# Attention whose value products are batched and turned round, page numbers clamped once, and streams that are never read

## What is computed

```python
def sb_attend(q, q_pos, k, v, k_pos):
    z = jnp.einsum('bthd,bshd->bhts', q, k).astype(jnp.float32) * HEAD_DIM ** -0.5
    mask = k_pos[None, :] < q_pos[:, None]
    log_1m = jnp.where(mask, jax.nn.log_sigmoid(-z), 0.0)
    suffix = lax.cumsum(log_1m, axis=3, reverse=True) - log_1m
    a = jnp.where(mask, jnp.exp(jax.nn.log_sigmoid(z) + suffix), 0.0)
    return jnp.einsum('bhts,bshd->bthd', a.astype(v.dtype), v)
...
    o_nsa = gates[..., 0:1] * o_cmp + gates[..., 1:2] * o_slc + gates[..., 2:3] * o_win
    mix = jnp.concatenate([rms_norm(o_nsa, g_on), rms_norm(o_sb, g_os)], axis=2).reshape(B, T, MIX_WIDTH)
    h = x + mix @ w_out
```

## Time and profile before

| | |
|---|---|
| runs | 3027.76, 3020.37 and 2997.0 us, median 3020.37 |
| profiled execution | 3020.68 us, of it a span of 3018.6 us from the first to the last instruction |
| mean granted clock of TensorE | 0.860 |
| busy over the span | TensorE 2675.0 us (89%), VectorE 1256.2 (42%), ScalarE 798.2 (26%), GpSimd 831.3 (28%) |
| attend, 682 to 1849 us | TensorE 1080.55 us busy at clock 0.75, VectorE 652.25, ScalarE 361.35, GpSimd 562.54 |
| decode_nsa, 1849 to 2040 us | TensorE 73.06 us busy at clock 0.65, VectorE 42.87, GpSimd 48.56 |

### The profile page before, as it was taken

How to read it: one execution, slowest core, us unless ns; L and a number is a source line. 1 busy time by engine, 2 the same in 40 slices (tenths; PEclk the granted TensorE clock), 3 DMA queues, 4 the chain that set the end, 5 groups by cost and what they waited for, 6 DMA issues and landing times. The chain is left out here.

```text
span 3018.6 us, 45708 instructions
## 1 busy us (share of the span) xinstructions
PE 2675.0 (89%) x13736; PEld 2003.8 (66%) x13736; DVE 1256.2 (42%) x2483; ACT 798.2 (26%) x1487; POOL 831.3 (28%) x845
## 2 busy tenths in 40 slices
PE   7989699983999999999999994357989999999999
PEld 6778677772765554555555551133469999999999
DVE  3463233332656566555566650223321111114553
ACT  4232133321333333332233330001121111113332
POOL 0120244403545545454455440412200000000000
PEclk9999789995569787776688797678999999999999
DMA  4224654408245545444465346313121111113200
GB/s 143 93 88 138 159 135 129 126 21 172 85 116 157 144 127 161 135 138 122 129 162 157 119 125 219 71 43 119 57 78 47 47 45 48 46 35 111 67 29 24
DMA packets 269781, 314.28 MB, mean 104 GB/s; under 512 B 62465, under 2 KB 177986, under 8 KB 269354
## 3 DMA queue, kind: packets, MB, share of 16 engines
q1 hardware_dynamic: 238842, 266.46, 30.3%
q0 software_dynamic: 14528, 38.32, 5.1%
q10 hardware_dynamic: 16192, 6.93, 0.9%
HBM read 278.89 MB, written 37.44 MB: 105 GB/s over the span
## 5 line engine op out<-in xcount | busy, mean ns | idle before, releaser
L1070 POOL TENSOR_TENSOR late<-late 128x512 f32<-128x512 f32 x256 | 336.7, 1318 | 280.3 <-DMA late<-in_cache_sb_kv 246.5
L1995 PE MATMUL pg<-h_turned_hi,w_gu_hi 128*128 128x344 f32 x1056 | 338.5, 321 | 10.2 <-DVE h_turned_lo L2043 10.2
L1997 PE MATMUL pg<-h_turned_hi,w_gu_lo 128*128 128x344 f32 x1056 | 338.4, 320 | 0.0
L1996 PE MATMUL pg<-h_turned_lo,w_gu_hi 128*128 128x344 f32 x1056 | 338.2, 320 | 0.0
L1190 PE MATMUL decode_ps<-late,weights_dec 128*8 128x512 f32 x512 | 312.6, 714 | 9.2 <-DMA late<-in_cache_sb_kv 8.0
L1241 ACT ACTIVATE probs<-scores,minus_max 128x63 f32<-128x63 f32 (+4 forms) x192 | 109.6, 571 | 604.2 <-DVE minus_max L1314 574.4
L2121 PE MATMUL py<-w_down_hi,act_hi 128*128 128x256 f32 x792 | 225.7, 285 | 9.8 <-DVE w_down_lo L2168 9.8
L2038 DVE TENSOR_TENSOR w_gu_lo<-late,w_gu_hi 128x512 fp32r<-128x512 f32 x88 | 61.0, 693 | 401.9 <-ACT w_gu_hi L2008 401.9
L2122 PE MATMUL py<-w_down_lo,act_hi 128*128 128x256 f32 x792 | 225.0, 284 | 0.0
L2123 PE MATMUL py<-w_down_hi,act_lo 128*128 128x256 f32 x792 | 225.0, 284 | 0.0
L2104 POOL DMA_DIRECT2D out_y_prompt<-y_rows x32 | 17.4, 545 | 744.5 <-DVE y_rows L2156 744.5
(11 more groups left out here) (281 smaller groups left out, 5360.0 us busy)
## 6 DMA issues: line engine op xcount, KB each, us to landing
late<-in_cache_sb_kv SPq DMA_DIRECT2D x512, 256.0 KB, 2.9
late<-in_w_gate_up SPq DMA_DIRECT2D x88, 256.0 KB, 2.9
late<-in_cache_nsa_kv SPq DMA_DIRECT2D x160, 128.0 KB, 3.8
late<-in_cache_nsa_kv POOLq DMA_DIRECT2D x96, 128.0 KB, 3.3
late<-in_w_down SPq DMA_DIRECT2D x4, 2816.0 KB, 10.9
w_in_raw<-in_w_in SPq DMA_DIRECT2D x40, 256.0 KB, 4.8
x_sb<-in_x_prompt SPq DMA_DIRECT2D x8, 512.0 KB, 3.9
out_sb_p<-proj_sb SPq DMA_DIRECT2D x16, 256.0 KB
```

The source lines that it names most:

```text
L1070: eng.tensor_tensor(prod[:, p % NPR], kr[:, p % RING], qb[:, u], ALU.mult).then_inc(multiplied, 1)
L1995: eng.matmul(pg[:, e, c, 0:CW], w_hi[:, h, j, :], hT_hi[:, k, cols], start=k == 0, stop=False)
L1996: eng.matmul(pg[:, e, c, 0:CW], w_hi[:, h, j, :], hT_lo[:, k, cols], start=False, stop=False)
L1997: mm = eng.matmul(pg[:, e, c, 0:CW], w_lo[:, h, j, :], hT_hi[:, k, cols], start=False, stop=k == KT - 1)
```

## The change

attend is written anew, and page numbers are treated differently in three stages.

- The loop is unrolled, and the order is that of BLOCK: 16 steps of two heads (u) and two neighbouring tiles (a), 16 blocks, 264 iterations.
- The values now stand in the array (64 columns) and the turned probabilities stream, 128 columns for sb and 256 for the others (two heads or two tiles of queries). Two products write rows 0 to 63 and rows 64 to 127 of `out_ps`: z is the head for sb, sel or win for the others, the tile for cmp. Five batches to a block, cut into pieces at the iterations of PV_AT. ScalarE copies a finished batch (`copy_out`), TensorE transposes it back (`turn_back`), VectorE scales it into `mix` (`finish`). The denominators come from the exponential's own sum (accum_out) instead of a 65th column.
- A value page of the samples is multiplied with weights padded to 32 columns, and four pages write rows 0 to 31, 32 to 63, 64 to 95 and 96 to 127 of `decode_ps`; the mask `diag` and the final sum run over 128 rows. The value ring has eight pages. Pages are spread over all 256 steps by a cost of each step (DEC), the last sample's value pages among them.
- `keep_streaming`: after the scores of each step of at most 512 columns (all of cmp, the others for tiles 0 to 3, 160 of 256 steps) two products of 384 columns, identity times masks, go into columns 512 to 895 of the same half of `scores`. Nobody reads them.
- VectorE saves one group of transposes in three, ScalarE two (before, half each). Queries are loaded in blocks of 256 columns by GpSimd, and v_sb by GpSimd instead of SyncE.
- SyncE loads eight page numbers at a time and doesn't check them. In compress VectorE clamps the page table once; in decode_nsa it clamps the block numbers; the checks of SyncE, ScalarE and GpSimd in these stages go.
- The copies of win_s_out move from decode_nsa to SyncE's queue in attend (sample 0, page 16), and the kv_win loads of decode_nsa behind ScalarE's first exponentials.

The diff, cut to its core:

```diff
-            _, numbers = nc.values_load_multi_w_load_instructions(pt[0:1, at + ids[0]:at + ids[-1] + 1], engines=[eng.engine], min_val=0, max_val=NPOOL - 1)
+            _, numbers = nc.values_load_multi_w_load_instructions(pt[0:1, at + ids[0]:at + ids[-1] + 1], engines=[eng.engine], min_val=0, max_val=NPOOL - 1, skip_runtime_bounds_check_because=CLAMPED)
...
+                eng.tensor_copy(ptf[:, :], pt[:, :])
+                eng.drain()
+                eng.tensor_scalar(ptf[:, :], ptf[:, :], 0.0, float(NPOOL - 1), ALU.max, ALU.min)
+                eng.drain()
+                eng.tensor_copy(pt[:, :], ptf[:, :]).then_inc(table_set, 1)
...
-        vr = late[:, 2048:4096].rearrange("p (r n) -> p r n", r=RING)
...
+        value_slot = lambda p: (vr_low, vr_high)[p % VRING // 4][:, p % 4]
...
-        aw = sb("weights_dec", [P, NH, NPAGE])
+        aw = sb("weights_dec", [P, 32, NPAGE])
...
+        BLOCK = [(0, 0, "sb"), (0, 0, "cmp"), (1, 0, "cmp"), (0, 1, "cmp"), (1, 0, "sb"), (1, 1, "cmp"), (0, 0, "sel"), (1, 0, "sel"),
+                 (0, 1, "sb"), (0, 0, "win"), (1, 0, "win"), (0, 1, "sel"), (1, 1, "sb"), (1, 1, "sel"), (0, 1, "win"), (1, 1, "win")]
+        STEPS = [(N, u, 2 * k + a, kind) for N in range(NBODY) for k in range(4) for u, a, kind in BLOCK]
...
-        KPAGES, VPAGES = spread((2, 2, 3, 4, 5, 5, 5, 6)), spread((0, 3, 3, 4, 5, 5, 6, 6))
...
-            body(0, 0)
-            with eng.Fori(1, 3) as i:
-                body(i, i - 1)
-            body(3, 1)
-            for s in range(H):
-                tail(s)
...
+        NBATCH = 5 * U // 16
+        PV_AT, OUT_AT = ((8,), (10, 11), (12, 13, 14), (18, 19), (20, 21, 22)), (9, 12, 15, 20, 23)
+        END = U - 16 + OUT_AT[4] + 1
...
+        cost = [0.9 + 0.4 * tiles_of(kind, t) for N, u, t, kind in STEPS]
+        DEC = [[] for _ in range(END)]
+        for n in range((NH + 1) * NPAGE):
+            goal, i, total = (n + 0.5) / ((NH + 1) * NPAGE) * sum(cost), 0, cost[0]
+            while total < goal:
+                i += 1
+                total += cost[i]
+            DEC[i].append((n // NPAGE, n % NPAGE))
+        VGROUP = {6: 0, 9: 1, 13: 2, 16: 3, 20: 4, 23: 5, 27: 6, 31: 7}
...
+                def numbers(h, p):
+                    _, found = nc.values_load_multi_w_load_instructions(pt[0:1, h * NPAGE + p:h * NPAGE + p + 8], engines=[eng.engine], min_val=0, max_val=NPOOL - 1, skip_runtime_bounds_check_because=CLAMPED)
+                    return found
...
-                    page = eng.value_load(pt[0:1, bass.ds(h * NPAGE + p, 1)], min_val=0, max_val=NPOOL - 1)
...
+                for h in range(NH + 1):
+                    for p0 in range(0, NPAGE, 8):
+                        key_ids = numbers(h, p0) if h < NH else None
+                        value_ids = numbers(h - 1, p0) if h else None
+                        for p in range(p0, p0 + 8):
+                            if h < NH:
+                                key_page(h, p, key_ids[p - p0])
+                            if h:
+                                value_page(h - 1, p, value_ids[p - p0])
+                            if p == 5 and h >= 2:
                                 store_row(h - 2)
-                            if p == 6 and not zero(h) and not (isinstance(h, int) and h == NH - 1):
-                                eng.wait_ge(pv_done, h * H)
-                                load_values(h + 1, 1 - u)
-
-                def tail(s):
-                    value_page(NH - 1, s)
-                    if s == 5:
-                        store_row(NH - 2)
-
-                turns(eng, body, tail)
+                            if p == 16 and h == 0:
+                                eng.dma_start(io["win_s_out"][:, 0:WINDOW - 1, :], io["state"][:, 1:WINDOW, :]).then_inc(row_stored_w, 16)
...
+                def keep_streaming(f):
+
+                    if width(STEPS[f][3], STEPS[f][2]) <= 512:
+                        for _ in range(2):
+                            eng.matmul(S[:, f % 2, 512:512 + 3 * P], identb[:, :], masks[:, :, :].rearrange("p m q -> p (m q)"), start=True, stop=True)
...
-                        mm = eng.matmul(O[:, 0:HD if kind == "sb" else HD + 1], l, r, start=c == 0, stop=c == tiles - 1)
...
+                def turn_back(bt):
+                    N, t, kind, W = batch(bt)
+                    eng.wait_ge(ot_saved, bt + 1)
+                    bank_free(("out", bt))
+                    for u in range(W // P):
+                        mm = eng.transpose(PT[:, bank_of["out", bt], u * P:(u + 1) * P], oT[:, bt % 2, u * P:(u + 1) * P], ident[:, :])
+                    mm.then_inc(out_turned, 1)
...
+                    count = (t + 1, t + 1 if kind == "sb" else tiles_of("win", t))
+                    for c in range((t + 1) * piece // pieces, (t + 1) * (piece + 1) // pieces):
+                        for z in range(2):
+                            if c >= count[z]:
+                                continue
+                            if kind == "sb":
+                                l, r = vs[:, z, c, :], prT[:, SB_SLOT + c, z * P:z * P + P]
+                            else:
+                                name = ("sel", "win")[z]
+                                l, r = vx[:, z, first_tile(name, t) + c, kv, :], prT[:, slot_of(name, t) + c, :]
+                            mm = eng.matmul(O[HD * z:HD * z + HD, 0:W], l, r, start=c == 0, stop=c == count[z] - 1)
...
-                            eng.matmul(DB[0:NH, :], aw[:, :, NPAGE - 1 - p], vr[:, p % RING], start=p == 0, stop=p == NPAGE - 1).then_inc(v_used, 1)
...
+                        for p in pages:
+                            eng.wait_ge(v_loaded[p % VRING], h * VPER - VPER + 16 * (p // VRING) + 16)
+                        for i, p in enumerate(pages):
+                            eng.matmul(DB[32 * i:32 * i + 32, :], aw[:, :, NPAGE - 1 - p], value_slot(p), start=p < SIDE, stop=p >= NPAGE - SIDE).then_inc(v_used, 1)
...
+                for i in range(END):
+                    if i < U:
+                        scores(i)
+                        keep_streaming(i)
+                    for bt, _ in at_iteration(i, OUT_AT):
+                        turn_back(bt)
+                    if 2 <= i < U + 2:
+                        transposes(i - 2)
+                    for bt, piece in at_iteration(i, PV_AT):
+                        product(bt, piece)
+                    for h, s in DEC[i]:
+                        sample(h, s)
...
-                    eng.activation(pr[:, s % 2, 0:w], S[:, s % 2, 0:w], ACT.Exp, bias=nm[:, s:s + 1]).then_inc(exp_done, 1)
...
+                    eng.activation(pr[:, f % 2, 0:w], S[:, f % 2, 0:w], ACT.Exp, bias=nm[:, f % 8:f % 8 + 1], accum_out=den[:, t, u, br:br + 1]).then_inc(exp_done, 1)
...
+                def copy_out(bt):
+                    N, t, kind, W = batch(bt)
+                    eng.wait_ge(pv_done, bt + 1)
+                    if bt >= 2:
+                        eng.wait_ge(out_turned, bt - 1)
+                    eng.activation(oT[:, bt % 2, 0:W], O[:, 0:W], ACT.Copy).then_inc(ot_saved, 1)
...
-                    eng.reciprocal(f, O[:, HD:HD + 1])
...
+                    eng.reciprocal(f4, den[:, t, :, 1:3])
...
-            _, found = nc.values_load_multi_w_load_instructions(block_id[0:1, 32 * b + a:32 * b + e], engines=[eng.engine], min_val=0, max_val=2 * NPOOL - 1)
+            _, found = nc.values_load_multi_w_load_instructions(block_id[0:1, 32 * b + a:32 * b + e], engines=[eng.engine], min_val=0, max_val=2 * NPOOL - 1, skip_runtime_bounds_check_because=CLAMPED)
...
-                eng.dma_start(io["win_s_out"][:, 0:WINDOW - 1, :], io["state"][:, 1:WINDOW, :]).then_inc(o_stored, 16)
-                eng.dma_start(io["win_s_out"][:, WINDOW - 1, :], io["win_new"]).then_inc(o_stored, 16)
...
-                for b in range(NB):
-                    eng.dma_start(wk[:, b], io["state"][b].rearrange("(t p) e -> p t e", p=P)).then_inc(state_loaded[b // SIDE], 16)
...
+                for b in range(NB):
+                    eng.dma_start(wk[:, b], io["state"][b].rearrange("(t p) e -> p t e", p=P)).then_inc(state_loaded[b // SIDE], 16)
...
-                eng.tensor_copy(block_id[:, :], PB[0:1, 256:256 + X * 16]).then_inc(ids_set, 1)
+                eng.tensor_scalar(idf[:, :], PB[0:1, 256:256 + X * 16], 0.0, float(2 * NPOOL - 1), ALU.max, ALU.min)
+                eng.drain()
+                eng.tensor_copy(block_id[:, :], idf[:, :]).then_inc(ids_set, 1)
```

640 lines of the change are left out of this document (342 added, 298 removed).

## The result

The changed kernel takes 2837.38 us (median of five runs, 2814.77 to 2844.85) against 3020.37 us: a ratio of 0.9412, 95% interval 0.9363 to 0.946. The forecast was 2641 us with a range of 2530 to 2830. The direction was right; the gain was 183 us instead of 379. The profiled execution is the shortest of the five, with a span of 2813.1 us, so sums within the profile come out some 22 us shorter than the median, and where the loop of another run is laid beside this one, that much of the difference belongs to this execution.

What follows compares the result with a forecast made beforehand. TensorE and its clock were taken to bound the loop. Loop -294, setup -8, tail -35, decode_nsa -40 and compress -3 sum to -380; 3018.6 - 380 + 2.1 = 2641 us, range 2530 to 2830.

Steps and rivals of the forecast that it cites:

- the loop's sum: Attention loop: TensorE's 677 us of work times 1.12 for waits, plus 27 us for the clock, gives 785 us.
- one block's 27 us for the clock: Attention loop: the first blocks still run at 1.2 GHz; one block's 27 us of work was put on that.
- the rule on weight loads: TensorE: weight loads overlap products only in different row groups; column tiles share theirs, so much of both gains would be lost.
- the range 629 to 725: Attention loop: TensorE's work at full clock after the change, 677 us with half the cost of changes of shape.
- the 183 from 860 to 677: Attention loop: TensorE's work at full clock falls from 860 us, eight heads of 107.5 us, to 677 us.
- the 48 us for changes of shape: Attention loop: 240 visits to column tiles, two shape changes each, cost TensorE 0 to 96 us; half was taken.
- rival A: Attention loop: streams don't hold the clock, blocks of tiles 0 to 3 stay at 1.2 GHz; +193, 2834 us; chance 0.14.
- rival D: Attention loop: TensorE's shorter work never brings the clock up, 0.50 throughout; 3210 us; chance 0.03.
- The 12%: Attention loop: waits on top of TensorE's 677 us, between 5 and 18%, giving 758 us.
- setup: Ahead of the loop: v_sb loads leave SyncE's queue and fewer operations stand there; -8 us, range 0 to -15.
- the tail: Behind the loop: the last head's value pages move into the loop, leaving 12 us instead of 47; -35 us.
- decode_nsa: Stage decode_nsa: earlier first exponentials, -14 us, and dropped checks, 8 x 3.2 = -26; sum -40 us (-20 to -55).

## Why the prediction was wrong

The step that failed is the loop's sum, "677 x 1.12 = 758 us", and one block's 27 us for the clock: 785 against 965 us in the profile. The prices of single instructions inside it came out 15 to 19% low, which isn't the main part.

- **Prices.** Eight page instructions in four tiles take 1.12 us (forecast 0.94). Sb products stand at twelve in about 0.8 us (1596.51 to 1597.32 in the row below), 0.068 us each, where 0.059 was taken. So column tiles overlap; the rule on weight loads that the prediction cited from the Trainium skill, "TensorE: Matmul & The Clock Gate", Part 3, doesn't make them serial in this kernel: four column tiles take 1.12 us, one takes 3.65.

```profile
1592.88 1.12 PE L1263 MATMUL decode_ps<-value_pages_high,weights_dec 128*32 128x512 f32 x8
...
1596.51 0.88 PE L1242 MATMUL out_ps<-probs_turned,v_sb 128*64 128x128 f32 x12
1597.32 0.29 PE L1158 MATMUL scores<-kc_prompt_hi,q_nsa_hi_twice 64*128 64x64 f32 x1
```

- **Work.** An estimate: 44% of 826 us of busy time at half clock, 363 us, are some 180 us of excess if all of it doubles; that leaves about 645 us at full clock, in the range 629 to 725. That it fits is partly luck. The same estimate gives some 784 us for the old loop (1046 x 0.75), where the prediction started from 860: its passes contain waits (95.0 us of work in the 98.8 of tiles 1 to 7), and it charged value pages to eight heads where the loop has those of seven. So the work fell by some 140 us, not by the 183 from 860 to 677; a start that was too high and a saving that was too large cancel. No run isolates the 48 us for changes of shape.
- **The clock term was mis-sized**, 27 us against about 180. I read the loss of the clock as a matter of the first blocks; rival A put it at tiles 0 to 3. Its time, 2834 us, is that of the result, but by accident: those blocks are at 0.79 on average, not 0.5, and about 280 of the loop's 430 us at half clock lie in the wide blocks. What had filled TensorE there are the page products, over three times shorter now: in the run that makes them long again the clock is higher in all eight wide blocks. That is the mechanism of rival D, which had been given 0.03, without its size: the loop's mean is 0.78, not 0.50.
- **The waits were mis-sized**, 139 us of idle time against 81. The 12% came from a pass of the kernel before. The new queue of copy, transpose back and bank didn't exist there, so no row of it could give that share.
- **Neither term can be added alone.** That is the deeper fault: the sum treats the loop as TensorE's work plus a share. The runs show a loop that also goes round through the other engines' in-order queues: 142 us of TensorE's work in the pages are worth 48, and with the same instructions on TensorE a sum moved in VectorE's queue is worth 50 us and lighter page work 81. TensorE's work isn't free in it either: of about 116 us of scores 84 came out of the time.

The other terms held: setup 31 us where 32 were expected (40 before), the tail some 7 instead of 12 us, compress about 6 us less (3 forecast). In decode_nsa ScalarE's first exponentials start 15 us after the stage's start (11 forecast), ScalarE's forty block loads, with three loads of numbers among them, take 38.83 instead of 46.31 us, so the checks cost some 2.5 us a sample and not 3.2, and the stage is about 34 us shorter (40 forecast). The waits for pages are 54.8 us on GpSimd, down from 246.5, so the page queue didn't become the bound. In the row of the first exponentials below, it is now the maximum that releases them, no longer the issue of the kv_win loads:

```profile
1692.39 0.47 ACT L1618 ACTIVATE late<-SD,nmx_cmp 128x255 f32<-128x255 f32 x1 [17.57 <-DVE nmx_cmp L1737]
...
1719.82 38.83 ACTq L1571 DMA_DIRECT2D kv_sel<-in_cache_nsa_kv  x40
```

What stays open is what holds the clock down in each block (the wait at 1601 us above is one case), how waits and clock share the loop's missing 180 us, and how long the loop would be at full clock throughout: no loop had a clock above 0.89, and streams that raise it take time themselves.

## What to carry to other kernels

When TensorE's work falls by a fifth, look for the engine order that its length used to hide: trace one pass through all the queues and ask what each waiting instruction holds behind it, before a share of waits is carried over from the old loop. A wait is worth less than its length where the next one is close behind, and an instruction that waits for another engine belongs behind the work on its queue that is ready. Price an added stream by what it leaves of TensorE's busy time, not by the clock: the same streams gave 2.7% where they took 82 us off it, and nothing where it stayed within 13 us.

## What was not expected of the hardware

320 products that nobody reads raise the mean granted clock of the old loop from 0.75 to 0.88 and shorten it from 1079 to 998 us, although they are themselves work for the busiest engine. In the changed kernel 1024 of them in place of 320 raise it from 0.78 to 0.89 with 17 us more busy time, so nearly the whole of some 120 us of work (an estimate) came out of the higher clock. And a shortened instruction can lower the clock for all the others: with pages in four column tiles instead of one the loop's clock is 0.78 instead of 0.86.
